# High and low parts of the rows as one 512-column operand in the FFN's first product, with its convolution taps read from SBUF

## The chip, the cores and the metric

The kernel runs on one core of a Trainium2 chip. The metric is the device time of one execution in microseconds (us); lower is better. Engines are called by the profile's names: PE is TensorE, DVE is VectorE, ACT is ScalarE, POOL is GpSimd, SP is SyncE, whose queue issues the weight loads.

## The reference, cut to what matters

One inference step of a hybrid backbone with four layers (mLSTM, windowed attention, neighbourhood attention, mLSTM) on 128 prompt tokens and 128 sample tokens, all in float32. Every layer ends with a gated feed-forward part (FFN) with a depthwise convolution of width 3 over the tokens between its first product and the gate:

```python
def _conv_ffn(h, w_up, conv_w, conv_b, w_down):
    u = _dwconv(h @ w_up, conv_w, conv_b)
    g, val = u[..., :D_FF], u[..., D_FF:]
    return (jax.nn.silu(g) * val) @ w_down
```

`D_MODEL` is 1024 and `D_FF` 2816, so `h @ w_up` is (256 x 1024) by (1024 x 5632) in each of the four layers, and the second product is (256 x 2816) by (2816 x 1024).

## The kernel before, in words

Activations lie transposed: features on the 128 partitions, the 256 tokens (two groups of 128, `TOK` in all) on the free axis. Every float32 product is made of three products of the narrower type float32r: a value is divided into a high part (`_hi`, a copy in float32r) and a low part (`_lo`, value minus high part), and w_hi·x_hi + w_hi·x_lo + w_lo·x_hi is summed in PSUM.

**Weights.** All weights are read once, in the order of use, as tiles of 1 MB (`stream`, 374 tiles) into a ring of four buffers `raw0` to `raw3`. SP issues the load of a tile into a buffer as soon as the tile that lay there has both its low halves made (`lo_done`), or, for the tiles of the conditioning product ("ada"), has been used by PE. Each other tile is split in two halves of 1024 columns: ACT writes the high part (`split_hi`, L446), DVE the low part (`split_lo`, L457), into a ring of `SPL` = 4 half-tile buffers `spl_hi` and `spl_lo`. A half-tile buffer comes free when PE has used the half (`half_used`), so the splits can be at most two tiles ahead of PE.

**FFN's first product.** For layer `i`, loop `j` runs over `NJ` = 11 pairs of tiles: tile `u` = 2j holds the weights of 256 gate features, tile 2j+1 those of 256 value features, each for all eight 128-row blocks of the input. `weights_stationary` (L534 to L536) does, for each of eight row blocks `k` and two blocks `b` of 128 features, three matmuls of 256 columns into one half of a PSUM bank: w_hi·H_hi, w_hi·H_lo, w_lo·H_hi; that is 48 matmuls a tile. `H_hi` and `H_lo` are the normalised input's parts, each 8 x 256 columns. The PSUM banks of the pair are `UP[0]`, `UP[1]` for even j and `ACC[2]`, `ACC[3]` for odd j.

**Behind the product.** ACT reads the finished bank and writes the middle tap with its bias to `tg` (gate) or `tv` (value) (`taps`, L1502, two instructions of 256 columns). DVE adds the two side taps, four `scalar_tensor_tensor` instructions for a tile, again with the PSUM bank as operand (`side_taps`, L1675 and L1679). ACT makes `sg` = silu(`tg`) (L1527), POOL multiplies `gt` = `sg`·`tv` (L2255), ACT writes `G_hi` (`gated_hi`), DVE writes `G_lo` (`gated_lo`, L2116). `G` is the operand of the second product, which `project` does (L585 to L587) in the same three-matmul form into `ACC[0]` to `ACC[3]`.

**Order.** Each engine's program is written out by hand in its own block, and its instructions run in that order; semaphores tie the engines. Per j, ACT's order is: split of tile 2j+1, taps of tile 2j, `gated_hi` of j-1, split of tile 2j+2, taps of tile 2j+1, silu. DVE's is: split of 2j+1, side taps of 2j, `gated_lo` of j-1, split of 2j+2, side taps of 2j+1. During layers 0 to 2 a few ada tiles (`fill`) run on PE between: one each after j = 2, 3 and 4, others around the norms. `norm` makes the input of each stage: DVE `hf` (L1626), POOL adds the shift (L2204), ACT `H_hi`, DVE `H_lo` (L1635), in four groups, and the first product's first tile waits for them group by group.

`H_hi`/`H_lo` are also read by the mLSTM's two input products (`weights_stationary`) and by the attention layers' `half_rows` (L567).

## Time and profile before

| | us |
|---|---|
| median of 3 runs | 1908.06 (1907.72 to 1908.47) |
| profiled execution | 1907.03 |
| its span in the trace | 1905.2 |

The profile page sums each engine's busy time over the span, cuts the span into 40 slices of 47.6 us, follows back the chain of work that ended last, and groups instructions by line. Durations of one instruction include its own start and end, so two that follow each other closely overlap in the record: where the pace matters, start times are compared, not durations. A matmul of 256 columns is recorded as 0.28 us long though the next one starts 0.12 us after it.

### The profile page before, as it was taken

The page shows a single profiled execution, that of the slowest core. Times are in us where ns is not written, and L with a number is a line of the kernel's source. Part 1 is how long each engine was busy: PE and PEld are TensorE (multiplying, and loading weights), DVE is VectorE, ACT ScalarE, POOL GpSimd, SP SyncE. Part 2 cuts the span into 40 slices and gives each one's busy share as a digit, 9 for nine tenths or more (in the row PEclk, how much of TensorE's full clock was granted, in tenths as well). Part 3 has the DMA queues.
Part 4 walks back from the last instruction along what each step waited for, and adds up shares of the span by engine and source line. Part 5 has one row for each costly group of instructions (what it writes and reads, how often), then busy time and mean ns, then how long its engine had stood idle before and what let it go on. Part 6 is the DMA issues. An engine that isn't in the chain of part 4 may idle for free.

```text
span 1905.2 us, 32196 instructions
## 1 busy us (share of the span) xinstructions
PE 1844.5 (97%) x13744; PEld 1652.7 (87%) x13744; DVE 1270.5 (67%) x1739; ACT 926.7 (49%) x1365; POOL 270.5 (14%) x198
## 2 busy tenths in 40 slices
PE   5999999999999999999999999999999999999998
PEld 2999877798999867999976789998998777989998
DVE  3854676667786666787455677856654776668874
ACT  2753445444554354555344455545643445446552
POOL 2100121011110122111111221102100220021211
PEclk8999999999999999999999999999999999999999
DMA  9555556857655767655573776556655647645551
GB/s 363 198 228 185 202 182 261 313 198 279 226 186 197 272 228 296 240 189 192 206 289 150 287 278 234 188 193 243 226 183 167 222 176 284 253 150 185 190 193 52
DMA packets 72543, 418.41 MB, mean 220 GB/s; under 512 B 12176, under 2 KB 18696, under 8 KB 24144
## 3 DMA queue, kind: packets, MB, share of 16 engines
q1 hardware_dynamic: 53856, 392.19, 55.4%
q10 hardware_dynamic: 18544, 24.17, 3.9%
q8 instruction: 108, 1.77, 0.4%
q14 instruction: 35, 0.29, 0.0%
HBM read 405.35 MB, written 10.95 MB: 218 GB/s over the span
## 4 chain that ended last, share of the span: by engine, by line
PE 87%; DVE 5%; DMA 2%; ACT 2%; issue 2%; POOL 2%; ACTq 0%; POOLq 0%; SPq 0%; DVEq 0%
PE ps L534 15%; PE ps L535 15%; PE ps L536 15%; PE ps L551 9%; PE ps L585 6%; PE ps L586 6%; PE ps L587 6%; PE ps L567 4%; PE ps L598 3%; DMA raw<-in_stream 2%; PE ps L801 1%; DVE spl_lo L457 1%; PE ps L786 1%; DMA out_new_C<-c_stage 1%; POOL hf L2204 1%
## 5 line engine op out<-in xcount | busy, mean ns | idle before, releaser
L457 DVE TENSOR_TENSOR spl_lo<-raw,spl_hi 128x1024 fp32r<-128x1024 f32 x556 | 726.8, 1342 | 249.2 <-ACT spl_hi L446 248.5
L446 ACT ACTIVATE spl_hi<-raw 128x1024 fp32r<-128x1024 f32 x556 | 565.1, 1053 | 305.5 <-PE ps L587 160.9
L534 PE MATMUL ps<-H_hi,spl_hi 128*128 128x256 f32 x1920 | 548.4, 286 | 8.3 <-DVE H_lo L1635 6.7
L535 PE MATMUL ps<-H_lo,spl_hi 128*128 128x256 f32 x1920 | 544.3, 283 | 0.0
L536 PE MATMUL ps<-H_hi,spl_lo 128*128 128x256 f32 x1920 | 544.2, 283 | 0.0
L534 PEld LDWEIGHTS ps<-H_hi,spl_hi 128*128 128x128 f32 x1920 | 369.4, 192 | 30.2 <-issue 30.1
L535 PEld LDWEIGHTS ps<-H_lo,spl_hi 128*128 128x128 f32 x1920 | 369.7, 193 | 0.1
L536 PEld LDWEIGHTS ps<-H_hi,spl_lo 128*128 128x128 f32 x1920 | 369.4, 192 | 0.0
L585 PE MATMUL ps<-G_hi,spl_hi 128*128 128x256 f32 x704 | 199.2, 283 | 0.0
L586 PE MATMUL ps<-G_lo,spl_hi 128*128 128x256 f32 x704 | 199.2, 283 | 0.0
L587 PE MATMUL ps<-G_hi,spl_lo 128*128 128x256 f32 x704 | 199.2, 283 | 0.0
L2255 POOL TENSOR_TENSOR gt<-sg,tv 128x512 f32<-128x512 f32 x44 | 92.7, 2106 | 439.9 <-DVE tv L1679 377.2
L534 PE MATMUL ps<-B_hi,spl_hi 128*128 128x256 f32 x512 | 145.0, 283 | 0.0
L535 PE MATMUL ps<-B_lo,spl_hi 128*128 128x256 f32 x512 | 144.9, 283 | 0.0
L536 PE MATMUL ps<-B_hi,spl_lo 128*128 128x256 f32 x512 | 144.9, 283 | 0.0
L585 PEld LDWEIGHTS ps<-G_hi,spl_hi 128*128 128x128 f32 x704 | 135.2, 192 | 0.0
L586 PEld LDWEIGHTS ps<-G_lo,spl_hi 128*128 128x128 f32 x704 | 135.2, 192 | 0.0
L587 PEld LDWEIGHTS ps<-G_hi,spl_lo 128*128 128x128 f32 x704 | 135.2, 192 | 0.0
L598 PE MATMUL ps<-raw,cond_wide 128*32 128x512 f32 x768 | 103.6, 644 | 20.4 <-DMA raw<-in_stream 10.8
L534 PEld LDWEIGHTS ps<-B_hi,spl_hi 128*128 128x128 f32 x512 | 98.3, 192 | 0.0
L536 PEld LDWEIGHTS ps<-B_hi,spl_lo 128*128 128x128 f32 x512 | 98.3, 192 | 0.0
L535 PEld LDWEIGHTS ps<-B_lo,spl_hi 128*128 128x128 f32 x512 | 98.3, 192 | 0.0
(237 smaller groups left out, 2754.2 us busy)
## 6 DMA issues: line engine op xcount, KB each, us to landing
raw<-in_stream SPq DMA_DIRECT2D x374, 1024.0 KB, 5.0
out_new_C<-c_stage ACTq DMA_DIRECT2D x16, 512.0 KB, 4.0
ada_b<-in_ada_b ACTq DMA_DIRECT2D x4, 768.0 KB, 9.9
E<-rows_out ACTq DMA_DIRECT2D x8, 256.0 KB, 4.5
Em<-rows_out ACTq DMA_DIRECT2D x8, 256.0 KB, 4.8
x<-in_x ACTq DMA_DIRECT2D x1, 1024.0 KB, 12.1
wide<-rows_out ACTq DMA_DIRECT2D x8, 128.0 KB, 5.5
cache<-in_na_cache ACTq DMA_DIRECT2D x1, 1024.0 KB, 7.9
```

The source lines that it names most:

```text
L446: act.activation(spl_hi[m % SPL][:, :], raw[r % RAW][:, h * HALF:(h + 1) * HALF], ACT.Copy).then_inc(S["hi_done"], 1)
L457: dve.tensor_tensor(spl_lo[m % SPL][:, :], raw[r % RAW][:, h * HALF:(h + 1) * HALF], spl_hi[m % SPL][:, :].bitcast(F32), ALU.subtract).the ...
L534: pe.matmul(out, w_hi, x_hi, start=st, stop=False, skip_group_check=True)
L535: pe.matmul(out, w_hi, x_lo, start=False, stop=False, skip_group_check=True)
L536: mm = pe.matmul(out, w_lo, x_hi, start=False, stop=en, skip_group_check=True)
L551: mm = pe.matmul(ACC[2 * s + c][:, :], a, w[m % SPL][:, c * 512:(c + 1) * 512], start=st, stop=en, skip_group_check=True)
L567: mm = pe.matmul(banks[s][:, :], a, w[m % SPL][:, k * 512:(k + 1) * 512], start=t == h == k == 0 and a is a_hi and w is spl_hi, stop=t == ...
L585: pe.matmul(out, w_hi, x_hi, start=st, stop=False, skip_group_check=True)
L586: pe.matmul(out, w_hi, x_lo, start=False, stop=False, skip_group_check=True)
L587: mm = pe.matmul(out, w_lo, x_hi, start=False, stop=en, skip_group_check=True)
L598: mm = pe.matmul(ADA_PS[32 * j:32 * j + ADA_M, 0:ADA_N], cond_wide[:, k * ADA_M:(k + 1) * ADA_M], raw[r % RAW][:, j * ADA_N:(j + 1) * ADA_ ...
L2255: pool.tensor_tensor(gt[j % 2][:, :], sg[j % 2][:, :], tv[j % 2][:, :], ALU.mult).then_inc(S["gt_done"], 1)
```

## The change: what it does

- `H_hi` and `H_lo` become one tensor `H` in which the high and low parts of each row block lie side by side: 256 columns high, 256 columns low. Its writers in `norm` write with a stride (`beside`), and the readers outside the FFN take their halves from it (`both_of`).
- The FFN's first product uses a new routine `wide_up`. For each row block and each block of 128 features it issues two matmuls in place of three: w_hi against all 512 columns (high and low part at once), and w_lo against the 256 high columns, accumulated on the first 256 of the 512 outputs. A feature block's output is now a whole bank, in two halves, and a tile takes two banks. Three such pairs of banks (`UPS`) are used in turn: `ps4`/`ps5`, `ps0`/`ps1`, `ps2`/`ps3`.
- The two halves of the output have to be added. ACT copies the high half of both banks to a new SBUF tile `up` (three buffers of 512 columns), DVE adds the low half from PSUM (`sum_up`). PE waits with tile u for the sum of tile u-3.
- The middle tap (ACT) and the side taps (DVE) read `up` in SBUF in place of the PSUM bank.
- The splits of tile u+2 are divided: its first half is split before the engine waits for tile u, its second half after the copy (ACT) or after the sum (DVE).
- The gate product `gt` = `sg`·`tv` moves from POOL to DVE, behind the side taps of the value tile.
- Not shown in the diff below: `split_hi` and `split_lo` get an argument that names the halves, two semaphores are added (`up_hi`, `up_sum`), and the three calls of `both(H_hi, H_lo)` outside the FFN become `both_of(H)`.

```diff
@@ -298,8 +298,7 @@
     x = sb("x", KD * TOK, F32, 64 * KB)
-    H_hi = sb("H_hi", KD * TOK, F32R, 72 * KB)
-    H_lo = sb("H_lo", KD * TOK, F32R, 80 * KB)
+    H = sb("H", 2 * KD * TOK, F32R, 72 * KB)
     rA, rB, rX, rT, rW = 88 * KB, 120 * KB, 152 * KB, 168 * KB, 184 * KB
@@ -340,6 +339,7 @@
                       for o, name in enumerate(("tg", "tv", "sg", "gt")))
+    up = [sb(f"up{b}", 2 * TOK, F32, rW + 2 * KB * b) for b in range(3)]
     G_hi = sb("G_hi", 2 * NJ * TOK, F32R, rA)
@@ -397,9 +397,11 @@
-    ps = [nc.alloc_psum_tensor(f"ps{b}", [P, 512], F32) for b in range(8)]
+    two = [nc.alloc_psum_tensor(f"ps{b}", [P, 1024], F32) for b in range(4)]
+    ps = [two[b // 2][:, 512 * (b % 2):512 * (b % 2) + 512] for b in range(8)]
     ACC, UP, ADA_PS, MISC = ps[0:4], ps[4:6], ps[6], ps[7]
     SCORES = (UP[1], MISC)
+    UPS = (two[2], two[0], two[1])
@@ -408,6 +410,13 @@
         return ap.rearrange("p (a b) -> p a b", b=b)
+    def halves(u):
+        return UPS[u % 3][:, :].rearrange("p (b e t) -> p b e t", e=2, t=TOK)
+    def beside(t, g, e):
+        return t[:, g * 1024:(g + 1) * 1024].rearrange("p (k e t) -> p k e t", e=2, t=TOK)[:, :, e]
@@ -536,6 +545,24 @@
+            def wide_up(n, banks, norm=None):
+                for h in range(2):
+                    m = 2 * n + h
+                    pe.wait_ge(S["lo_done"], m + 1)
+                    for k in range(4):
+                        kk = 4 * h + k
+                        if norm is not None and k % 2 == 0:
+                            pe.wait_ge(S["h_done"], 4 * norm + 2 * h + k // 2 + 1)
+                        for b in range(2):
+                            c = slice(k * 256 + b * P, k * 256 + b * P + P)
+                            w_hi, w_lo = spl_hi[m % SPL][:, c], spl_lo[m % SPL][:, c]
+                            pe.matmul(banks[:, b * 512:(b + 1) * 512], w_hi, H[:, kk * 512:(kk + 1) * 512], start=kk == 0,
+                                      stop=False, skip_group_check=True)
+                            mm = pe.matmul(banks[:, b * 512:b * 512 + TOK], w_lo, H[:, kk * 512:kk * 512 + TOK],
+                                           start=False, stop=kk == KD - 1, skip_group_check=True)
+                    mm.then_inc(S["half_used"], 1)
             def rows_stationary(n, chunk, first, last):
@@ -1048,14 +1078,12 @@
                 for j in range(NJ):
-                    k = NJ * i + j
-                    g_bank, v_bank = (ACC[2], ACC[3]) if j % 2 else (UP[0], UP[1])
-                    if j >= 2:
-                        pe.wait_ge(S["cg_done"], k - 1)
-                    weights_stationary(n0 + 2 * j, both(H_hi, H_lo), 0, g_bank, True, True, 2 * i + 1 if j == 0 else None)
-                    if j >= 2:
-                        pe.wait_ge(S["cv_done"], k - 1)
-                    weights_stationary(n0 + 2 * j + 1, both(H_hi, H_lo), 0, v_bank, True, True)
+                    for u in range(2 * j, 2 * j + 2):
+                        if u >= 3:
+                            pe.wait_ge(S["up_sum"], 2 * NJ * i + u - 2)
+                        elif u == 1 and i + 1 == DEPTH:
+                            pe.wait_ge(S["cn_evac"], 8 * MH)
+                        wide_up(n0 + u, UPS[u % 3], 2 * i + 1 if u == 0 else None)
                     if i + 1 < DEPTH:
@@ -1126,7 +1154,7 @@
                     act.wait_ge(S["hf_done"], 4 * q + g + 1)
-                    copy(H_hi[:, g * 512:(g + 1) * 512], hf[g % 2][:, :], "hhi_done")
+                    copy(beside(H, g, 0), v3(hf[g % 2][:, :], TOK), "hhi_done")
                     if late and g == 1:
@@ -1496,11 +1524,11 @@
-                def taps(dst, bank, j, blk, sem):
+                def taps(dst, u, blk, sem):
+                    act.wait_ge(S["up_sum"], 2 * NJ * i + u + 1)
                     for b in range(2):
-                        k = blk + 2 * j + b
-                        act.activation(dst[:, b * TOK:(b + 1) * TOK], bank[:, b * TOK:(b + 1) * TOK], ACT.Identity,
-                                       bias=small[:, b0 + k:b0 + k + 1],
+                        o, k = slice(b * TOK, (b + 1) * TOK), blk + u // 2 * 2 + b
+                        act.activation(dst[:, o], up[u % 3][:, o], ACT.Identity, bias=small[:, b0 + k:b0 + k + 1],
                                        scale=small[:, w0 + k:w0 + k + 1]).then_inc(S[sem], 1)
@@ -1510,22 +1538,28 @@
+                def high(u):
+                    split_hi(act, n0 + u + 2, (0,))
+                    tile_used(act, n0 + u)
+                    if 2 * NJ * i + u >= 3:
+                        done = NJ * i + (u - 3) // 2 + 1
+                        act.wait_ge(S[("cg_done", "cv_done")[(u - 3) % 2]], done)
+                    copy(v3(up[u % 3][:, :], TOK), halves(u)[:, :, 0], "up_hi")
+                    split_hi(act, n0 + u + 2, (1,))
+                split_hi(act, n0 + 1)
                 for j in range(NJ):
                     k = NJ * i + j
-                    g_bank, v_bank = (ACC[2], ACC[3]) if j % 2 else (UP[0], UP[1])
-                    split_hi(act, n0 + 2 * j + 1)
-                    tile_used(act, n0 + 2 * j)
-                    taps(tg[j % 2], g_bank, j, 0, "tg_done")
+                    high(2 * j)
+                    taps(tg[j % 2], 2 * j, 0, "tg_done")
                     if j:
                         gated_hi(j - 1)
-                    split_hi(act, n0 + 2 * j + 2)
-                    tile_used(act, n0 + 2 * j + 1)
+                    high(2 * j + 1)
                     if k >= 2:
                         act.wait_ge(S["gt_done"], k - 1)
-                    taps(tv[j % 2], v_bank, j, FB // 2, "tv_done")
+                    taps(tv[j % 2], 2 * j + 1, FB // 2, "tv_done")
                     act.wait_ge(S["cg_done"], k + 1)
                     act.activation(sg[j % 2][:, :], tg[j % 2][:, :], ACT.Silu).then_inc(S["sg_done"], 1)
-                split_hi(act, INDEX["ffn_down", i, 1])
                 gated_hi(NJ - 1)
@@ -1632,8 +1666,8 @@
                     dve.wait_ge(S["hhi_done"], 4 * q + g + 1)
-                    dve.tensor_tensor(H_lo[:, g * 512:(g + 1) * 512], hf[g % 2][:, :],
-                                      H_hi[:, g * 512:(g + 1) * 512].bitcast(F32), ALU.subtract).then_inc(S["h_done"], 1)
+                    dve.tensor_tensor(beside(H, g, 1), v3(hf[g % 2][:, :], TOK), beside(H, g, 0).bitcast(F32),
+                                      ALU.subtract).then_inc(S["h_done"], 1)
@@ -2116,23 +2150,35 @@
+                def sum_up(u):
+                    split_lo(dve, n0 + u + 2, (0,))
+                    dve.wait_ge(S["up_hi"], 2 * NJ * i + u + 1)
+                    t = v3(up[u % 3][:, :], TOK)
+                    dve.tensor_tensor(t, halves(u)[:, :, 1], t, ALU.add).then_inc(S["up_sum"], 1)
+                    split_lo(dve, n0 + u + 2, (1,))
+                split_lo(dve, n0 + 1)
                 for j in range(NJ):
                     k = NJ * i + j
-                    g_bank, v_bank = (ACC[2], ACC[3]) if j % 2 else (UP[0], UP[1])
-                    split_lo(dve, n0 + 2 * j + 1)
+                    sum_up(2 * j)
+                    dve.wait_ge(S["tg_done"], 2 * k + 2)
+                    side_taps(tg[j % 2], up[2 * j % 3], 2 * j, w0, w0 + 2 * FB, "cg_half", 2 * k + 2, "cg_done")
+                    if j:
+                        gated_lo(j - 1)
                     if i + 1 < DEPTH:
...
                             mod_columns(i + 1, 0)
-                    dve.wait_ge(S["tg_done"], 2 * k + 2)
-                    side_taps(tg[j % 2], g_bank, 2 * j, w0, w0 + 2 * FB, "cg_half", 2 * k + 2, "cg_done")
-                    if j:
-                        gated_lo(j - 1)
-                    split_lo(dve, n0 + 2 * j + 2)
+                    sum_up(2 * j + 1)
                     dve.wait_ge(S["tv_done"], 2 * k + 2)
-                    side_taps(tv[j % 2], v_bank, FB // 2 + 2 * j, w0, w0 + 2 * FB, "cv_half", 2 * k + 2, "cv_done")
-                split_lo(dve, INDEX["ffn_down", i, 1])
+                    side_taps(tv[j % 2], up[(2 * j + 1) % 3], FB // 2 + 2 * j, w0, w0 + 2 * FB, "cv_half", 2 * k + 2,
+                              "cv_done")
+                    dve.wait_ge(S["cv_done"], k + 1)
+                    dve.wait_ge(S["sg_done"], k + 1)
+                    if k >= 2:
+                        dve.wait_ge(S["ghi_done"], k - 1)
+                    dve.tensor_tensor(gt[j % 2][:, :], sg[j % 2][:, :], tv[j % 2][:, :], ALU.mult).then_inc(S["gt_done"], 1)
                 gated_lo(NJ - 1)
@@ -2246,13 +2292,6 @@
-                for j in range(NJ):
-                    k = NJ * i + j
-                    pool.wait_ge(S["sg_done"], k + 1)
-                    pool.wait_ge(S["cv_done"], k + 1)
-                    if k >= 2:
-                        pool.wait_ge(S["glo_done"], k - 1)
-                    pool.tensor_tensor(gt[j % 2][:, :], sg[j % 2][:, :], tv[j % 2][:, :], ALU.mult).then_inc(S["gt_done"], 1)
             norm(2 * DEPTH, shift=False)
```

## Rows read from the trace of the kernel before

**Rows 1.** The page: busy time of each engine, and the span in 40 slices.
```profile
PE 1844.5 (97%) x13744; PEld 1652.7 (87%) x13744; DVE 1270.5 (67%) x1739; ACT 926.7 (49%) x1365; POOL 270.5 (14%) x198
PE   5999999999999999999999999999999999999998
```

**Rows 2.** The page: chain of work that ended last, share of the span by engine.
```profile
PE 87%; DVE 5%; DMA 2%; ACT 2%; issue 2%; POOL 2%; ACTq 0%; POOLq 0%; SPq 0%; DVEq 0%
```

**Rows 3.** Stages: stretch, us, PE, PEld, DVE, ACT, POOL busy (instructions), PEclk, DMA share, GB/s.
```profile
442.90:574.20 131.30, 131.30 (x1093) 128.38 (x1090) 106.53 (x145) 75.13 (x109) 23.12 (x12) 1.00 0.61 225
1700.60:1830.50 129.90, 129.90 (x1071) 129.90 (x1072) 107.36 (x145) 76.80 (x113) 23.94 (x12) 0.99 0.51 180
```

**Rows 4.** Timeline of ACT in layer 0: start, us; taps of three tiles in turn.
```profile
568.08 1.02 ACT L1502 ACTIVATE tg<-ps,small 128x256 f32<-128x256 f32 x2 [2.33 <-PE ps L536]
569.52 2.00 ACT L446 ACTIVATE spl_hi<-raw 128x1024 fp32r<-128x1024 f32 x2
573.84 1.02 ACT L1502 ACTIVATE tv<-ps,small 128x256 f32<-128x256 f32 x2 [2.33 <-PE ps L536]
```

**Rows 5.** Timeline of PE, first product, layer 0: first and last of 57 matmuls.
```profile
454.72 0.28 PE L536 MATMUL ps<-H_hi,spl_lo 128*128 128x256 f32 x1
...
461.44 0.28 PE L535 MATMUL ps<-H_lo,spl_hi 128*128 128x256 f32 x1
```

**Rows 6.** Timeline of PE, mLSTM's value product: first start to last, ten pairs of matmuls.
```profile
200.02 0.62 PE L551 MATMUL ps<-spl_lo,A_hi 128*128 128x512 f32 x2
...
204.55 0.62 PE L551 MATMUL ps<-spl_hi,A_lo 128*128 128x512 f32 x2
```

**Rows 7.** Timeline of DVE over one pair j in layer 0; in brackets the idle time before.
```profile
563.38 0.87 DVE L1675 SCALAR_TENSOR_TENSOR tv<-ps,small,tv 128x254 f32<-128x254 f32 x2 [1.11 <-ACT tv L1502]
564.29 0.87 DVE L1679 SCALAR_TENSOR_TENSOR tv<-ps,small,tv 128x254 f32<-128x254 f32 x2
565.07 3.45 DVE L457 TENSOR_TENSOR spl_lo<-raw,spl_hi 128x1024 fp32r<-128x1024 f32 x2
569.14 0.87 DVE L1675 SCALAR_TENSOR_TENSOR tg<-ps,small,tg 128x254 f32<-128x254 f32 x2 [0.62 <-ACT tg L1502]
570.05 0.87 DVE L1679 SCALAR_TENSOR_TENSOR tg<-ps,small,tg 128x254 f32<-128x254 f32 x2
570.83 0.68 DVE L2116 TENSOR_TENSOR G_lo<-gt,G_hi 128x512 fp32r<-128x512 f32 x1
571.43 2.35 DVE L457 TENSOR_TENSOR spl_lo<-raw,spl_hi 128x1024 fp32r<-128x1024 f32 x2
```

**Rows 8.** Groups by line, all of the span: count, busy us, mean ns, idle before.
```profile
L1101 ACT ACTIVATE A_hi<-ps 128x512 fp32r<-128x512 f32 x16 | 9.6, 598 | 23.6 <-PE ps L536 23.6
L1842 DVE TENSOR_TENSOR E<-E,small 128x256 f32<-128x256 f32 x16 | 6.0, 417 | 0.0
L1986 DVE TENSOR_TENSOR O_lo<-ps,O_hi 128x256 fp32r<-128x256 f32 x16 | 6.8, 423 | 10.6 <-ACT O_hi L1101 10.6
L1857 DVE TENSOR_TENSOR den<-ps,den 128x512 f32<-128x512 f32 x8 | 5.5, 691 | 0.3
```

**Rows 9.** Waits of PE: who waited for whom, us in total, times, longest.
```profile
PE ps L534 <- DVE H_lo L1635: 6.7, 5, 2.7
PE ps L534 <- DVE spl_lo L457: 1.4, 5, 0.5
```

**Rows 10.** Timeline at the start of layer 3's FFN: its last low parts, its first tap.
```profile
1703.69 1.36 DVE L1635 TENSOR_TENSOR H_lo<-hf,H_hi 128x512 fp32r<-128x512 f32 x2 [1.20 <-ACT H_hi L1101]
1707.95 1.02 ACT L1502 ACTIVATE tg<-ps,small 128x256 f32<-128x256 f32 x2 [1.72 <-PE ps L536]
```

**Rows 11.** Stretches at the start of layer 1's FFN: PEclk, DMA share, GB/s.
```profile
752.00:754.00 2.00, 1.00 1.04 438
762.00:764.00 2.00, 1.00 1.05 436
```

More of the change, by code:

```diff
@@ L422, in build @@
         z_silu z_mul z_hi z_lo
-        tg_done cg_half cg_done tv_done cv_half cv_done sg_done gt_done ghi_done glo_done
+        up_hi up_sum tg_done cg_half cg_done tv_done cv_half cv_done sg_done gt_done ghi_done glo_done
         cache_landed bias_landed row_a row_d row_k row_v roped tq_mm tq_a tq_d tk_mm tk_a tk_d kv_landed
@@ L434, in landed, with split_hi @@
         eng.wait_ge(raw_landed[n % RAW], 16 * (n // RAW + 1))
-    def split_hi(act, n):
+    def split_hi(act, n, halves=(0, 1)):
         if n >= len(MAIN):
@@ L441, in split_hi @@
         landed(act, r)
-        for h in range(2):
+        for h in halves:
             m = 2 * n + h
@@ L447, in split_hi, with split_lo @@
                            ACT.Copy).then_inc(S["hi_done"], 1)
-    def split_lo(dve, n):
+    def split_lo(dve, n, halves=(0, 1)):
         if n >= len(MAIN):
@@ L453, in split_lo @@
         r = POS[MAIN[n]]
-        for h in range(2):
+        for h in halves:
             m = 2 * n + h
@@ L564, in half_rows @@
                         for s in range(NS):
-                            a_hi, a_lo = both(H_hi, H_lo)(4 * t + 2 * h + k, s)
+                            a_hi, a_lo = both_of(H)(4 * t + 2 * h + k, s)
                             for a, w in ((a_hi, spl_hi), (a_hi, spl_lo), (a_lo, spl_hi)):
@@ L622, in both, with both_of @@
                 return lambda k, s=None: (col(hi, k, s), col(lo, k, s))
+            def both_of(t):
+                return lambda k, s=None: (col(t, 2 * k, s), col(t, 2 * k + 1, s))
             def square_sums(q):
@@ L669, in mlstm @@
                     pe.wait_ge(S["conv_done"], 8 * j + t + 1)
-                    weights_stationary(n0 + t, both(H_hi, H_lo), 0, UP[t % 2], True, True,
+                    weights_stationary(n0 + t, both_of(H), 0, UP[t % 2], True, True,
                                        2 * i if t == 0 else None)
@@ L725, in gate_z @@
                     pe.wait_ge(S["z_silu"], 8 * j + t + 1)
-                    weights_stationary(INDEX["ml_z", i, t], both(H_hi, H_lo), 0, UP[t % 2], True, True)
+                    weights_stationary(INDEX["ml_z", i, t], both_of(H), 0, UP[t % 2], True, True)
                 pe.wait_ge(S["den_done"], 4 * (j + 1))
```

## The prediction

> **What bounds the kernel now.** I read the page first: PE is busy for 97% of the span and every slice but the first and the last has PE at 9 tenths [rows 1]. The chain that ended last runs over PE for 87% of the span; the rest is spread over five engines [rows 2]. Then the stage that is changed: in layer 0's first product PE is busy for all of the 131.3 us, DVE for 107, ACT for 75, and the same in layer 3 [rows 3]. The taps of successive tiles start 5.76 us apart, and ACT waits for PE each time [rows 4]; that is 48 matmuls at 0.120 us, the pace at which PE starts them: 56 steps in 461.44 - 454.72 = 6.72 us [rows 5]. So PE bounds the stage with no gap, at its full granted clock (1.00, 2.4 GHz) [rows 3]. A pair j takes 2 x 5.76 = 11.52 us.
>
> **PE: three matmuls become two.** The cost of a matmul is its pace, not its recorded length. 256 columns: 0.1200 us. At 2.4 GHz the columns alone are 0.1067, so 0.0133 is a part that belongs to each instruction. 512 columns, from the value product whose operands have the same types and the same 128 x 128 stationary: 20 matmuls in 204.55 - 200.02 = 4.53 us, 0.2265 each [rows 6]; the columns are 0.2133, and 0.0132 remains. So the fixed part is the same for both widths, and the change does the same columns (768) with one fixed part less. A group goes from 3 x 0.1200 = 0.3600 to 0.2265 + 0.1200 = 0.3465, a saving of 0.0135. There are 16 groups in a tile, 22 tiles in a layer, 4 layers: 1408 x 0.0135 = **19.0 us**. A tile goes from 5.76 to 5.544 us, a pair j to 11.09. No row has a 512-column matmul followed by a 256-column one with another stationary; from both sides the group costs between 0.333 (the next weights' load hides the fixed part in the longer stream, both parts gone: saving 38 us) and 0.360 or a little over (no saving). I take 0.3465, since its two halves are each measured.
>
> The Trainium skill (TensorE: Matmul & The Clock Gate, "Wait — 56ns, not 53.3ns?") gives a fixed cost of about 2.5 ns for a warm matmul. By that page the sum would be 1408 x 2.5 ns = 3.5 us, which would hardly be seen. This trace's rows show 13 ns instead, at both widths, and the sum goes by them.
>
> **What takes a part of it back.** The first tile of a layer waits for `H_lo` group by group [rows 9]. In layer 3 the last two low parts end at about 1704.4 and 1705.05, and the first tap starts at 1707.95 [rows 10], so that tile is paced by the norm and not by PE in its first half. There only the groups after the last wait are saved. I take 0.1 us lost a layer, **0.4 us**. Layers 1 and 2 start with the DMA engines full (438 and 436 GB/s) [rows 11]. A tile of 1 MB then takes 2.4 us, against 5.5 us for which PE works on one, and ACT's next wait in the stretch was for PE; the half split that is now earlier on ACT asks for a tile half a tile earlier. I cost it at nothing; the cover is the two tiles of lead that the four half buffers give. If it goes, the copy of tile u stands behind a wait for a load on ACT, 1 to 2 us in three layers, which the rotation of three bank pairs still hides.
>
> **DVE: does it keep up with 11.09?** From the starts over one j [rows 7]: 11.52 us, less the idle 1.11 and 0.62, is 9.79 us occupied. Removed: the two splits that run while POOL multiplies take 3.45 us, the two that do not 2.35, so moving the product off POOL gives DVE 1.10 back: 8.69. Added: two sums and one gate product of 512 elements. The row for this shape is `G_lo`, which occupies DVE from 570.83 to 571.43, 0.60 us; with a PSUM operand it is as long (691 ns for `den` against 682 for `G_lo`) [rows 7, 8]. So 3 x 0.60 = 1.80, and about 0.1 for the wait of the gate product on the side taps just before it: 10.6 us. Reading `up` in place of PSUM changes nothing for DVE: 417 ns from SBUF and 423 from PSUM for 256 elements [rows 8]. The bound on the other side is full durations with nothing overlapped, four splits at 1.23, eight taps at 0.478, four at 0.69 = 11.5. PE needs 11.09, and I take 10.6, by the row that shows the overlap: DVE has 0.5 us a pair left, and the work is hidden behind PE.
>
> **The waits that are new on DVE and ACT.** Behind PE's end of tile u: ACT copies (0.6 us, as in the copy of 512 columns from PSUM [rows 8]), DVE adds (0.7), meanwhile ACT splits the second half (1.0), DVE makes its low part (1.2, after a gap of 0.4 for ACT), ACT's two taps run beside that, DVE's side taps take 1.7. Queued behind DVE's wait for the copy are the low split of the second half and the side taps, for which PE waits later. The low part of half 1 of tile u+2 is ready 0.6 + 1.0 + 1.2 + small = 2.9 us after tile u; PE wants it after one and a half tiles, 8.3 us. The slack is 5.4 us. When DVE lags, ACT runs ahead with copy and split and the gap of 0.4 closes, so the chain doesn't repeat serially. PE's own new wait, for the sum of tile u-3, is two tiles (11 us) old when it comes. ACT: 75.1 us in 131.3 [rows 3], plus 22 copies of 0.6 and some 0.03 a tap = 90 in 122, no bound. SP: `raw` buffers are released about 2 us earlier than now. POOL is idle in the stage. In the pairs with `copy_mod` and `mod_columns` (j = 5 and 7) DVE has 0.7 to 0.8 more, that is 0.2 to 0.3 over one pair, taken up by the slack. After the last tile `G_lo` is complete about 6.6 us later (sum, split, side taps, product, high part, low part); the second product asks for it after two and a half tiles, 14.4 us. The writes to `H` with a stride change no element count: nothing, and if it were 0.1 us a group, 0.1 x 4 x 8 = 3 us on the path of the norms.
>
> **Sum.** 1907.03 - 19.0 + 0.4 = 1888.4 for an execution like the profiled one (span 1886.6). The median lies 1.03 above that execution, so 1889.5.
>
> **The rivals.**
> *Slower: DVE becomes the bound of the stage.* If a pair j takes x on DVE (or on the pair of ACT and DVE with their four hand-overs), a layer's first product takes 11x - 5.4 in place of 11 x 11.09. From x = 11.58 it costs something, from x = 12.0 all of the gain is gone. It would be 12.2 if no instruction overlapped (11.5 above) and both gaps of about 0.38 stayed: 4 x (11 x 1.11 - 5.4) = 27 us over the forecast, 1917. For it: DVE's busy time in the stage is 107 of 131 us already, and 1.8 us a pair are put on it. Against it: rows 7 show the overlap, and the POOL contention that goes. Chance 0.09.
> *Half of that: x between 11.6 and 12.0.* PE stalls in some pairs: 1890 to 1904. Chance 0.11.
> *The fixed part is not saved*, since it belongs to the hand-over between two stationaries or to the bank and the mixed widths pay it whole, or in truth it is near the page's figure: 0 to 3.5 us off, 1904.5 to 1908. For it: no row shows the mixture. Against: both widths show the same 13 ns. Chance 0.06.
> *The forecast*, 1887 to 1892: 0.71. *More than forecast* (the load of weights hides better beside 512 columns), 1870 to 1887: 0.03.
>
> **How the numbers follow.** About 0.2% (3.8 us) is what a measurement of this kernel can tell from no change, so faster means below 1904.2: 0.71 + 0.11 + 0.03 = 0.85. Same 0.06, slower 0.09. The range reaches from 1886 over the forecast and most of the half case to 1899; about 0.19 is left out.
>
> **What the profile of the changed kernel would show.** Matmuls of 512 and 256 columns in turn, starting 0.2265 and 0.120 apart; copies of ACT 5.54 us apart, each waiting for PE; PE busy in the whole of the stage, and the stage of layer 0 about 126.6 us in place of 131.3. Splits on DVE of 2.35 for two everywhere in it, none of 3.45; DVE busy about as now or a little more, with an idle rest of some 0.5 us a pair. The prediction is wrong if PE shows waits for `spl_lo` or `up` inside the stage (rival one, and their sum says how much), or if the groups start 0.36 us apart (the fixed part not saved).

## The result, and the profile after

The changed kernel takes 1893.15 us (median of 5, 1892.68 to 1898.71) against 1908.06. The ratio is 0.9923, with a 95% interval of 0.9913 to 0.9934: 14.7 us faster (12.6 to 16.6). It was forecast at 1889.5, with 1886 to 1899 as the range. So the direction and most of the size came as forecast, and about 4 us of the 18.6 are missing. The profiled execution is the slowest of the five (1898.71, span 1896.9), so the sum is not read from its span but stage by stage.

The page of the changed kernel: each engine's busy time (PEld is PE's loading of weights), and the two matmuls that took the place of three (line, engine, out<-in, shapes, count, busy us, mean ns, idle before).

```profile
PE 1835.8 (97%) x12336; PEld 1577.7 (83%) x12336; DVE 1312.5 (69%) x1871; ACT 980.9 (52%) x1453; POOL 177.7 (9%) x154
L560 PE MATMUL ps<-H,spl_hi 128*128 128x512 f32 x1408 | 497.5, 399 | 3.4 <-DVE H L1669 3.4
L562 PE MATMUL ps<-H,spl_lo 128*128 128x256 f32 x1408 | 393.9, 280 | 0.0
```

PE has the 1408 instructions less that the change removes [rows 1], and is as busy as before: it still bounds the kernel. In the stage (446 to 567 us, layer 0) the stretches show PE with no gap and DVE at 91%, where it was 81% [rows 3]:

```profile
446.00:567.00 121.00, 121.00 (x696) 102.69 (x697) 110.19 (x168) 85.23 (x124) 1.30 (x2) 1.00 0.62 237
```

The groups by line of the same stretch, DVE's and ACT's part:

```profile
L466 DVE TENSOR_TENSOR spl_lo<-raw,spl_hi 128x1024 fp32r<-128x1024 f32 x42 | 51.2, 1221 | 7.5 <-ACT spl_hi L455 7.3
L455 ACT ACTIVATE spl_hi<-raw 128x1024 fp32r<-128x1024 f32 x43 | 45.1, 1051 | 7.3 <-DMA raw<-in_stream 6.8 <-PE ps L562 0.2
L2157 DVE TENSOR_TENSOR up<-ps,up 128x512 f32<-128x512 f32 x20 | 13.7, 687 | 0.9 <-ACT up L1129 0.8
L2181 DVE TENSOR_TENSOR gt<-sg,tv 128x512 f32<-128x512 f32 x10 | 6.9, 693 | 0.3
```

The splits are at 1221 ns each, and none is stretched any more in any layer. DVE has 10.8 us idle in all (121.00 less 110.19), 7.5 of them before a split: about 1.0 us a pair. ACT waits 6.8 us for loads, which were costed at nothing; in layers 0 and 2 one copy comes 0.5 and 0.8 us late for that, and PE doesn't stall.

**Where the 4 us are.** ACT's copies mark the ends of tiles. Two places of layer 0, from the timeline of ACT (start, us, engine, line, operation):

```profile
463.10 0.60 ACT L1129 ACTIVATE up<-ps 128x512 f32<-128x512 f32 x1 [1.65 <-PE ps L562]
468.75 0.60 ACT L1129 ACTIVATE up<-ps 128x512 f32<-128x512 f32 x1 [1.66 <-PE ps L562]
...
545.74 0.60 ACT L1129 ACTIVATE up<-ps 128x512 f32<-128x512 f32 x1 [1.21 <-PE ps L562]
551.28 0.60 ACT L1129 ACTIVATE up<-ps 128x512 f32<-128x512 f32 x1 [1.34 <-PE ps L562]
```

Both wait for PE; the first pair is 5.65 us apart, the second 5.54. There are two paces. The timeline of PE, behind the first place and ahead of the second:

```profile
469.61 0.40 PE L560 MATMUL ps<-H,spl_hi 128*128 128x512 f32 x1
469.85 0.28 PE L562 MATMUL ps<-H,spl_lo 128*128 128x256 f32 x1
469.97 0.40 PE L560 MATMUL ps<-H,spl_hi 128*128 128x512 f32 x1
...
544.85 0.39 PE L560 MATMUL ps<-H,spl_hi 128*128 128x512 f32 x1
545.08 0.27 PE L562 MATMUL ps<-H,spl_lo 128*128 128x256 f32 x1
545.19 0.40 PE L560 MATMUL ps<-H,spl_hi 128*128 128x512 f32 x1
```

Averaged over the start times of 34 and of 97 groups, the 256-column matmul starts 0.2365 us after the 512-column one in the slow pace and 0.231 in the fast one, and the next 512-column one 0.117 and 0.1155 after it (starts are printed to 0.01 us; each part is good to about 0.001). A group takes 0.3533 or 0.3466 us. The forecast was 0.3465 everywhere. The loads of the weights do not tell the paces apart: in both each is recorded as 0.19 us long and starts within some 5 ns of a matmul's start. At the slow pace a tile keeps half of its gain. In this trace all of layer 3 is slow, layers 0 and 1 are slow up to the four transposes of the conditioning (`mod_rows`) after tile 13 and fast behind them, and layer 2 is fast at first, slow in the middle, fast at the end.

### The profile page after: what moved, and what is told of

It reads as the page before. It is cut to its first block, busy times and chain, and to the rows that moved or that the text cites. A ratio compares the mean times of both kernels' runs of the same rounds, so it can differ in the third digit from the quotient of the medians.

```text
span 1896.9 us, 29734 instructions
## 1 busy us (share of the span) xinstructions
PE 1835.8 (97%) x12336; PEld 1577.7 (83%) x12336; DVE 1312.5 (69%) x1871; ACT 980.9 (52%) x1453; POOL 177.7 (9%) x154
## 4 chain that ended last, share of the span: by engine, by line
PE 88%; DVE 5%; DMA 2%; ACT 2%; issue 2%; POOL 1%; ACTq 0%; POOLq 0%; SPq 0%; DVEq 0%
PE ps L560 17%; PE ps L578 9%; PE ps L562 9%; PE ps L612 6%; PE ps L614 6%; PE ps L613 6%; PE ps L543 6%; PE ps L545 6%; PE ps L544 6%; PE ps L594 4%; PE ps L625 3%; DMA raw<-in_stream 2%; DVE spl_lo L466 1%; PE ps L831 1%; PE ps L816 1%
## 5 line engine op out<-in xcount | busy, mean ns | idle before, releaser
L466 DVE TENSOR_TENSOR spl_lo<-raw,spl_hi 128x1024 fp32r<-128x1024 f32 x556 | 687.7, 1259 | 275.3 <-ACT spl_hi L455 274.3
L455 ACT ACTIVATE spl_hi<-raw 128x1024 fp32r<-128x1024 f32 x556 | 573.9, 1052 | 327.0 <-PE ps L614 161.5
L560 PE MATMUL ps<-H,spl_hi 128*128 128x512 f32 x1408 | 497.5, 399 | 3.4 <-DVE H L1669 3.4
L562 PE MATMUL ps<-H,spl_lo 128*128 128x256 f32 x1408 | 393.9, 280 | 0.0
L560 PEld LDWEIGHTS ps<-H,spl_hi 128*128 128x128 f32 x1408 | 265.0, 188 | 78.2 <-issue 14.6
L562 PEld LDWEIGHTS ps<-H,spl_lo 128*128 128x128 f32 x1408 | 266.1, 189 | 0.0
L543 PE MATMUL ps<-H,spl_hi 128*128 128x256 f32 x512 | 148.2, 289 | 6.8 <-DVE H L1669 5.2
L544 PE MATMUL ps<-H,spl_hi 128*128 128x256 f32 x512 | 146.0, 285 | 0.0
L545 PE MATMUL ps<-H,spl_lo 128*128 128x256 f32 x512 | 146.0, 285 | 0.0
L543 PEld LDWEIGHTS ps<-H,spl_hi 128*128 128x128 f32 x512 | 99.4, 194 | 16.6 <-issue 16.5
L1129 ACT ACTIVATE up<-ps 128x512 f32<-128x512 f32 x88 | 52.7, 599 | 115.5 <-PE ps L562 115.3
L544 PEld LDWEIGHTS ps<-H,spl_hi 128*128 128x128 f32 x512 | 99.5, 194 | 0.1
```

Source lines behind the costliest of these rows:

```text
L455: act.activation(spl_hi[m % SPL][:, :], raw[r % RAW][:, h * HALF:(h + 1) * HALF], ACT.Copy).then_inc(S["hi_done"], 1)
L466: dve.tensor_tensor(spl_lo[m % SPL][:, :], raw[r % RAW][:, h * HALF:(h + 1) * HALF], spl_hi[m % SPL][:, :].bitcast(F32), ALU.subtract).the ...
L543: pe.matmul(out, w_hi, x_hi, start=st, stop=False, skip_group_check=True)
L544: pe.matmul(out, w_hi, x_lo, start=False, stop=False, skip_group_check=True)
L545: mm = pe.matmul(out, w_lo, x_hi, start=False, stop=en, skip_group_check=True)
L560: pe.matmul(banks[:, b * 512:(b + 1) * 512], w_hi, H[:, kk * 512:(kk + 1) * 512], start=kk == 0, stop=False, skip_group_check=True)
```

## The experiments

"Stage sum" is the time from the first to the last copy of a layer (in the kernel before, to the last first tap), added over the four layers: 84 steps between tiles, with the fills and transposes that stand between them. It is 495.75 us in the kernel before and 483.2 in the first trace of the changed one. It leaves out everything that varies elsewhere; the spans outside it differ from trace to trace by up to 7 us (1408.3 to 1415.3) over all kernels, so times of single runs scatter by some 3 us either way. Each kernel has one trace; a pace is read from that one execution.

**The changed kernel again** (no edit). 

> The changed kernel once more. In its first trace the groups of two matmuls of the first product start 0.3533 us apart in some tiles (5.65 us a tile) and 0.3466 in others (5.55), and the pace changes only where PE did other work between. Theory A (the pace is set by how PE enters the stream of alternating widths, and holds until something interrupts it): this trace shows the same two values and no third, over long stretches, perhaps in other layers than before; runs lie between 1888.5 (all tiles at 0.3466) and 1898 (all at 0.3533), and the ratio is near 0.992. Theory B (slow tiles are slowed by what DVE and ACT do beside them): the same tiles are slow as before, since the work beside them is the same.

Measured: 1894.37 us (1892.93 to 1895.26), ratio 0.9921 (0.9909 to 0.9934). The stage sum is 480.6. The same two values, but in other places: layer 3, which was slow from end to end (118.7 us), is fast from end to end (116.5). Two of its copies (timeline of ACT), 5.54 us apart:

```profile
1739.94 0.60 ACT L1129 ACTIVATE up<-ps 128x512 f32<-128x512 f32 x1 [1.52 <-PE ps L562]
1745.48 0.60 ACT L1129 ACTIVATE up<-ps 128x512 f32<-128x512 f32 x1 [1.55 <-PE ps L562]
```

The instructions beside it are the same in both. Theory B falls in its simple form; the pace is a property of the execution, not of the tile.

**Three matmuls in the new layout.**

```diff
-                            pe.matmul(banks[:, b * 512:(b + 1) * 512], w_hi, H[:, kk * 512:(kk + 1) * 512], start=kk == 0,
-                                      stop=False, skip_group_check=True)
+                            pe.matmul(banks[:, b * 512:b * 512 + TOK], w_hi, H[:, kk * 512:kk * 512 + TOK], start=kk == 0,
+                                      stop=False, skip_group_check=True)
+                            pe.matmul(banks[:, b * 512 + TOK:(b + 1) * 512], w_hi, H[:, kk * 512 + TOK:(kk + 1) * 512],
+                                      start=False, stop=False, skip_group_check=True)
```

> The changed kernel, but with w_hi against 256 high columns and then 256 low columns in two matmuls in place of one of 512: three matmuls of 256 a group as in the kernel before, in the new layout, with the new banks, copies, sums, taps from SBUF and the product on DVE. Theory A (all of the gain is in the matmuls, all the rest is hidden behind PE): groups start 0.3600 us apart in every tile, 5.76 us a tile, and the time is that of the kernel before within 2 us, 1906 to 1910. Theory B (the new work on DVE and ACT costs PE something): slower than the kernel before by more than 2 us, or tiles of more than 5.76 us without a fill in them.

Measured: 1908.83 us (1906.62 to 1910.41), ratio 1.0004 (0.9995 to 1.0013), every tile without a fill at 5.76, stage sum 495.72 against 495.75. Two copies in layer 3 (timeline of ACT):

```profile
1744.16 0.60 ACT L1131 ACTIVATE up<-ps 128x512 f32<-128x512 f32 x1 [1.76 <-PE ps L564]
1749.92 0.60 ACT L1131 ACTIVATE up<-ps 128x512 f32<-128x512 f32 x1 [1.76 <-PE ps L564]
```

With the old matmuls all the rest of the change (copies, sums, taps from SBUF, product on DVE, interleaved `H`, divided splits, three bank pairs) is worth nothing in either direction, within 2 us. The whole gain is the instruction that is left out of each group. With one width only there is one pace.

**The order of the matmuls: by two, by four, by eight.** All 512-column matmuls of one, two or four row blocks first, then the 256-column ones; for one row block:

```diff
                         for b in range(2):
...
-                            pe.matmul(banks[:, b * 512:(b + 1) * 512], w_hi, H[:, kk * 512:(kk + 1) * 512], start=kk == 0,
-                                      stop=False, skip_group_check=True)
-                            mm = pe.matmul(banks[:, b * 512:b * 512 + TOK], w_lo, H[:, kk * 512:kk * 512 + TOK],
-                                           start=False, stop=kk == KD - 1, skip_group_check=True)
+                            pe.matmul(banks[:, b * 512:(b + 1) * 512], spl_hi[m % SPL][:, c], H[:, kk * 512:(kk + 1) * 512],
+                                      start=kk == 0, stop=False, skip_group_check=True)
+                        for b in range(2):
+                            c = slice(k * 256 + b * P, k * 256 + b * P + P)
+                            mm = pe.matmul(banks[:, b * 512:b * 512 + TOK], spl_lo[m % SPL][:, c], H[:, kk * 512:kk * 512 + TOK],
+                                           start=False, stop=kk == KD - 1, skip_group_check=True)
```

> The order of the matmuls alone is changed: for each row block the two of 512 columns first (both banks), then the two of 256 columns. Theory A: the slow pace comes from the change of width; with half as many changes of width either the slow pace is 0.0033 us a group dearer than the fast one in place of 0.0067, or it doesn't occur at all; 1888.5 to 1893. Theory B (work beside): the same two paces, 0.3533 and 0.3466, in the same tiles; 1893. A third possibility, that two matmuls of 512 in a row leave less room to load weights, would give a pace above 0.3533, 1899 or more.

> The order of the matmuls alone: of two row blocks the four of 512 columns first, then the four of 256. In pairs (two and two) a group took 0.3483 us in every tile, where the alternating order takes 0.3466 or 0.3533. Theory C (the sum of the two widths' own paces, 0.2265 and 0.1200, holds within a run of one width, and every change of width costs something fixed): half the surplus of 0.0017 is left, 0.3474 a group, 5.56 us a tile in all tiles, and no second pace. If the surplus doesn't depend on the number of changes: 0.3483 again. Time 1889 to 1894.

> The same with a whole half tile: eight of 512 columns, then eight of 256. By theory C 0.3470 a group, 5.552 us a tile in all tiles. The first tile of a layer has to wait for four groups of the norm at once and loses up to 1.4 us a layer where PE waits for them (the first tile in layer 3 above all). Time 1889 to 1894.

| order | us (median, range) | ratio (interval) | tile, us | group, us | stage sum |
|---|---|---|---|---|---|
| alternating, first trace | 1893.15 (1892.7 to 1898.7) | 0.9923 (0.9913 to 0.9934) | 5.65 or 5.55 | 0.3533 or 0.3466 | 483.2 |
| by two | 1897.65 (1891.7 to 1898.1) | 0.9932 (0.9920 to 0.9945) | 5.573 | 0.3483 | 480.3 |
| by four | 1898.02 (1896.5 to 1898.3) | 0.9938 (0.9925 to 0.9950) | 5.613 | 0.3508 | 483.3 |
| by eight | 1897.67 (1896.7 to 1899.5) | 0.9939 (0.9927 to 0.9952) | 5.587 | 0.3492 | 480.6 |

Each of the three has a single pace in its trace, so the second pace belongs, as far as these traces go, to the strict alternation. Theory C falls: fewer changes of width make a group dearer (by four) and not cheaper, and none reaches the fast alternating pace. That pace is the sum of the two single widths' own (0.3465 [rows 5, 6]), so grouping by width has nothing to give here. All three times lie above what was expected for them (at most 1893, 1894 and 1894). They are not shown to differ from the alternating order either: the intervals of the ratios overlap, and the stage sums lie, to 0.1 us, among those of the alternating kernels without added work (478.6 to 483.2). Whether the time outside the stage has a part in it is open (1413.3 to 1415.3 us in these three traces, 1409.6 to 1413.7 in the alternating ones without added work); by four and by eight also make the first tile of a layer wait for two or four groups of the norm at once.

**The order within a group turned**: w_lo against 256 columns, then w_hi against 512 (the two `matmul` calls change places, with the start flag). 

> The order within a group is turned: w_lo against 256 columns first, then w_hi against 512. A stream of alternating widths as before, so by theory A two paces again, 0.3466 and 0.3533 a group, with changes only where other PE work stands between; 1890 to 1897. If the second pace belongs to the order in which the same PSUM columns are written, there is one pace only.

Measured: 1894.37 us (1891.90 to 1897.35), ratio 0.9926 (0.9911 to 0.9941). Two paces again, 5.66 only in the first tiles of layer 1, 5.55 elsewhere; with 478.6 the shortest stage sum of all: 17.1 us less than before, of 17.9 that would be there with all 84 steps fast. It shows what the forecast's term is worth when the pace holds. Its traced execution is the fastest of its four (1891.90); the median shows no difference from the order as it was. The second pace does not belong to the order within a group.

**Other PE work between the tiles.** In layer 3 no fill stands between tiles, so its pace ought to change only where something is put in.

```diff
                         wide_up(n0 + u, UPS[u % 3], 2 * i + 1 if u == 0 else None)
+                        if i + 1 == DEPTH and u in NUDGE:
+                            pe.wait_ge(S["modT_done"], 3 * DEPTH)
+                            for b in range(NUDGE[u]):
+                                pe.transpose(ADA_PS[:, b * P:(b + 1) * P], ident, ident)
```

`NUDGE` is `{3: 1, 6: 1, 9: 2, 12: 2, 15: 4, 18: 4}`. 

> In layer 3 alone, where no other PE work stands between the tiles, PE does 1, 1, 2, 2, 4 and 4 transposes of 128 columns into an unused bank after tiles 3, 6, 9, 12, 15 and 18. They cost about 0.06 us each, 0.9 us in all. Theory A (entry into the stream sets the pace): the tiles' distance changes between 5.65 and 5.55 us at some of these places and at no other. Theory B (work beside them): it stays at 5.65 through all of layer 3, as in the first trace.

Measured: 1896.29 us (1893.16 to 1897.04), ratio 0.9928 (0.9913 to 0.9943). ACT's copies around the two places with two transposes (timeline of ACT, layer 3):

```profile
1744.34 0.60 ACT L1134 ACTIVATE up<-ps 128x512 f32<-128x512 f32 x1 [1.55 <-PE ps L563]
...
1749.88 0.60 ACT L1134 ACTIVATE up<-ps 128x512 f32<-128x512 f32 x1 [1.52 <-PE ps L563]
...
1755.76 0.60 ACT L1134 ACTIVATE up<-ps 128x512 f32<-128x512 f32 x1 [1.71 <-PE ps L563]
...
1761.41 0.60 ACT L1134 ACTIVATE up<-ps 128x512 f32<-128x512 f32 x1 [1.66 <-PE ps L563]
...
1772.85 0.60 ACT L1134 ACTIVATE up<-ps 128x512 f32<-128x512 f32 x1 [1.65 <-PE ps L563]
1778.39 0.60 ACT L1134 ACTIVATE up<-ps 128x512 f32<-128x512 f32 x1 [1.55 <-PE ps L563]
```

5.54 apart ahead of the first place, 5.88 over it, 5.65 behind it, and 5.54 again behind the second. One transpose left the pace as it was (two of two), two changed it (two of two), four led to the slow pace, from the fast one and from the slow one. A transpose cost 0.11 us, and not 0.06 as expected. In layer 3 the pace changed nowhere else. That bears out theory A: other work of PE can change the pace, and it then holds until something interrupts the stream. Whether it is the kind of work or only the length of the interruption is not separated here.

**Four transposes with an increment.** 

> After the first tile of every layer, and in layer 3 after tiles 7 and 14 too, PE does four transposes of 128 columns into an unused bank, the last with a semaphore increment, as the transposes of the conditioning (mod_rows) have it after tile 13 of layers 0 to 2. In the seven traces of the alternating order looked at so far, all 21 stretches behind mod_rows ran at 5.55 us a tile, though the tiles before ran at either pace, while four transposes without an increment left 5.65 in both of two cases. Theory D (the increment, or four transposes ended in this way, puts PE into the fast pace): 5.55 behind each of the six places. Theory A alone (any entry, either pace by chance): both values among the six. The transposes cost some 0.4 us each time, 2.4 us in all; time 1890 to 1898.

Measured: 1897.93 us (1894.44 to 1898.84), ratio 0.9944 (0.9928 to 0.9961). Behind the six places: slow in layers 0, 1 and 2, fast behind the first in layer 3, slow behind the other two. Theory D falls. Behind `mod_rows` the pace was fast once more, in 24 of 24 stretches of the eight traces (in that of `load1`, below, for one step, until DVE set the pace). An entry that took either pace by chance would not do that, and what makes this one different is open. Four transposes cost 0.44 us each time. Had they forced the fast pace, they would have gained 0.1 us net over the five tiles up to the first fill in layers 0 to 2, and 1.8 us in layer 3, where all of it slow takes 118.7 us and all of it fast 116.5.

**More work on DVE.** Behind the sum of each tile:

```diff
                     dve.tensor_tensor(t, halves(u)[:, :, 1], t, ALU.add).then_inc(S["up_sum"], 1)
+                    dve.tensor_tensor(ow[1][:, :], x[:, 0:512], x[:, 512:1024], ALU.add)
```

> The changed kernel with one more DVE instruction of 512 elements for each tile, behind the sum (its output is used by nothing), 0.6 us or 1.2 us a pair. The prediction has DVE occupied for x = 10.6 us a pair and says that PE begins to lose at x = 11.58, with 4 x (11 x (x - 11.09) - 5.4) us. By it x = 11.8 and the load costs 9.6 us over the changed kernel, somewhat less since PE's tiles took 5.60 us on the mean in the traces so far (5 us at 11.2 a pair): 1898 to 1904. If DVE has in truth more room than that (x of 10.2 or less without the load), nothing is lost and the time is 1892 to 1896. If DVE were already the bound, the whole load would show: 88 x 0.6 = 53 us.

Measured: 1899.73 us (1897.43 to 1902.71), ratio 0.9954 (0.9938 to 0.9971), 6.6 us over the changed kernel's median (6 us by the ratios). Tiles run at 5.55 or 5.65 us up to about the eighth (layer 3) or the sixteenth (layers 0 to 2) and at 5.84 from there. The timeline of DVE over one pair in layer 3, from one sum to the next but one:

```profile
1746.84 0.69 DVE L2157 TENSOR_TENSOR up<-ps,up 128x512 f32<-128x512 f32 x1
1747.44 0.69 DVE L2159 TENSOR_TENSOR ow<-x 128x512 f32<-128x512 f32 x1
1748.03 1.22 DVE L466 TENSOR_TENSOR spl_lo<-raw,spl_hi 128x1024 fp32r<-128x1024 f32 x1
1749.17 0.88 DVE L1709 SCALAR_TENSOR_TENSOR tv<-up,small,tv 128x254 f32<-128x254 f32 x2
1750.08 0.88 DVE L1713 SCALAR_TENSOR_TENSOR tv<-up,small,tv 128x254 f32<-128x254 f32 x2
1750.99 0.69 DVE L2183 TENSOR_TENSOR gt<-sg,tv 128x512 f32<-128x512 f32 x1
...
1758.51 0.68 DVE L2157 TENSOR_TENSOR up<-ps,up 128x512 f32<-128x512 f32 x1
```

No row has a bracket, nor has any of those left out: DVE is never idle for 0.15 us or more, and a pair takes 1758.51 - 1746.84 = 11.67 us. Less the two added instructions at 0.60 that is x = 10.47; the forecast put 10.6. A stretch a little later in the same layer is a warning:

```profile
1770.00:1820.00 50.00, 49.98 (x286) 43.31 (x284) 49.58 (x78) 34.31 (x52) 0.00 (x0) 1.00 0.49 177
```

PE is busy for 49.98 of 50 us although DVE sets its pace: the waits are shorter than the tail by which one recorded matmul overlaps the next (a 512-column one is recorded as 0.40 us long, the next starts after 0.23). "PE has no gap" doesn't show by itself that PE is the bound; the distance of its tiles does.

The same with one instruction of 1024 elements (`spare[:, :]` from `x[:, 0:1024]` and `x[:, 1024:2048]`). 

> The same with one instruction of 1024 elements for each tile, 1.1 to 1.2 us or 2.3 us a pair. By the prediction's formula x = 12.9 and the cost is 4 x (11 x 1.8 - 5.4) = 58 us over the changed kernel, 1950, and in the stage DVE has no idle time and PE waits for spl_lo or up. With room of another 0.5 us a pair it would be 35 us, 1928.

Measured, one run: 1941.51 us, 48 over the changed kernel's median; a pair takes 12.74 us in the trace (tiles of 6.37). From the waits of PE:

```profile
PE ps L561 <- DVE spl_lo L467: 17.6, 33, 0.8
```

Only here does a wait for DVE inside the stage become visible. x without the load is 12.74 - 2 x 1.13 = 10.5 once more.

**The product back on POOL** (the block removed from POOL's program put back, DVE's instruction taken out). 

> The changed kernel with the gate product back on POOL. DVE loses 0.7 us of work a pair and gets back the 1.1 that its splits lose while POOL multiplies: x = 11.0 by the prediction, still below 11.09. Theory A: PE bounds the stage either way, the time is that of the changed kernel within 2 us (1891 to 1896), and the splits of 1.7 us a piece are back in the trace. Rival: the move is worth something on the path since x is over 11.6 without it; then slower by 3 us or more, with waits of PE for spl_lo inside the stage.

Measured: 1892.35 us (1890.86 to 1896.85), ratio 0.9924 (0.9907 to 0.9941): no difference, as theory A has it. But its second half is mostly wrong: of the 38 stretched splits of the kernel before (over 1.5 us, in the four stages) 4 are back, none in layers 0 and 3. One line's summary (min/median/max ns), in the kernel before over layer 0's stage and here, and POOL and DVE beside each other here:

```profile
L457 DVE TENSOR_TENSOR spl_lo<-raw,spl_hi x44: 1212/1220/2320, 446.2 to 572.6; 128x1024 fp32r<-128x1024 f32 x44
```

```profile
L466 DVE TENSOR_TENSOR spl_lo<-raw,spl_hi x44: 1215/1221/1226, 447.0 to 566.1; 128x1024 fp32r<-128x1024 f32 x44
541.61 2.17 POOL L2296 TENSOR_TENSOR gt<-sg,tv 128x512 f32<-128x512 f32 x1 [9.56 <-DVE tv L1713]
541.39 1.22 DVE L466 TENSOR_TENSOR spl_lo<-raw,spl_hi 128x1024 fp32r<-128x1024 f32 x1
542.96 0.69 DVE L2157 TENSOR_TENSOR up<-ps,up 128x512 f32<-128x512 f32 x1 [0.35 <-ACT up L1129]
543.91 1.23 DVE L466 TENSOR_TENSOR spl_lo<-raw,spl_hi 128x1024 fp32r<-128x1024 f32 x1 [0.25 <-ACT spl_hi L455]
```

The split that starts 0.2 us ahead of POOL's product takes its 1.22 us; the next DVE instruction in POOL's 2.17 us is the sum, which has an operand in PSUM, and it takes its 0.69. The next split starts when POOL has ended. In the kernel before, two splits followed each other there, and the second started inside POOL's instruction and took 2.32. The same happens here in layer 1, where a split starts 0.15 us behind POOL; and in layer 0 there is a product with no split beside it (a second POOL row of this trace):

```profile
812.28 1.29 POOL L2296 TENSOR_TENSOR gt<-sg,tv 128x512 f32<-128x512 f32 x1 [11.30 <-DVE tv L1713]
812.43 2.22 DVE L466 TENSOR_TENSOR spl_lo<-raw,spl_hi 128x1024 fp32r<-128x1024 f32 x1 [0.28 <-ACT spl_hi L455]
481.71 1.30 POOL L2296 TENSOR_TENSOR gt<-sg,tv 128x512 f32<-128x512 f32 x1 [9.14 <-DVE tv L1713]
```

So it is an instruction that starts while POOL works and reads two operands in SBUF that is held up. And it goes both ways: POOL's product takes 1.3 us by itself and 2.15 when a split is already running as it starts, in nearly all pairs of the kernel before. The Trainium skill says so (SBUF — State Buffer, "Who interferes with whom": a VectorE instruction with two SBUF inputs contends with a GpSimd instruction that reads SBUF), and these traces agree: 2.32 us against 1.22 for the split, and 0.69 for the sum with its PSUM operand. In the new order of DVE the move off POOL returns next to nothing; it costs DVE 0.6 to 0.7 us a pair, which PE covers.

**Undivided splits.**

```diff
-                    split_hi(act, n0 + u + 2, (0,))
                     tile_used(act, n0 + u)
...
-                    split_hi(act, n0 + u + 2, (1,))
+                    split_hi(act, n0 + u + 2)
```

and the same for `split_lo` around the sum. 

> The changed kernel with the splits undivided: both halves of tile u+2 behind the copy and behind the sum. The low part of half 0 comes 1.1 us later, with 2.8 us less slack, since PE wants it after one tile. Theory A: hidden, same time within 2 us (1891 to 1896), the DVE's idle time a little longer. Rival: the divided split is what keeps PE fed, then PE waits for spl_lo, 3 us or more slower.

Measured: 1893.71 us (1892.26 to 1896.42), ratio 0.9928 (0.9914 to 0.9943), stage sum 482.3: no difference. The division is worth nothing as long as PE is the bound.

## Why the prediction was right, and where it was off

- **PE bounds the stage and the gain is in the matmuls:** shown, by `three` (1.0004 with the old matmuls and all the rest new).
- **The fixed part of 0.0133 us an instruction, 1408 of them, 19.0 us:** that a group with one instruction less is cheaper is right; this is the term that was mis-sized. It assumed that the paces measured in streams of one width add up in a mixed stream. In the fast pace they do (0.3466 against 0.3465), but by a sum whose parts are not the forecast's: the starts lie 0.231 and 0.1155 apart, where 0.2265 and 0.120 were forecast, and none of the other patterns gives the sum (0.3483, 0.3508, 0.3492, and 0.3533 in the slow pace, where only 0.0067 is saved). How exactly the fast pace meets it may be luck. In the traces of the alternating order that have no added work the stage sums are 12.5, 15.2, 13.5, 13.5 and 17.1 us under the kernel before's, 14.4 on the mean; the forecast has 18.1 for these 84 steps. The 3.8 us between them are about the 4 us that the time misses. The prediction said that no row had the mixture and gave 0.333 to 0.360 as the ends, and took the middle for likely. It did not think of two values in one execution. Layer 0's first product was forecast to take 4.7 us less (126.6 in place of 131.3); from its first matmul to the start of ACT's first work on its last tile it takes 127.6 in place of 131.0, 3.3 less.
- **The 2.5 ns a matmul of the Trainium skill** (TensorE: Matmul & The Clock Gate, "Wait — 56ns, not 53.3ns?"): an estimate of 3.5 us by that page. The stage gained 12.5 to 17.1. The rows decided rightly.
- **DVE at x = 10.6:** 10.5 by `load1` and `load2`. Its parts were not all right: the 1.1 us were counted as returned by moving the product; without the move nearly all of them would have come back too, through the new order. The loss beyond the slack was mis-sized at its lower end. At x = 11.67 the formula gives 4 us with PE at 11.09 a pair and nothing with PE at the 11.2 it really took; 6 to 7 were measured. At 12.74 it gives 51 and 46; 48 were measured. The lead of 5.4 us a layer is what is too large: in layer 3 of `load1` the tiles slow down after eight steps, when DVE has fallen behind by 8 x (5.84 - 5.55) = 2.3 us, and in `load2` by 3.1 us. In the other layers, as an estimate from the same steps, the fills between the tiles (1.2 us of PE's time each) let DVE catch up, which the formula leaves out.
- **What is hidden:** copies, taps, ACT's waits for loads, the divided split: at nothing, and nothing, within 2 us, is what `three` and `whole` show. The writes to `H` with a stride were not tested by themselves; `three` contains them. The prediction read [rows 11] as the starts of layers 1 and 2; both rows are of layer 1.
- **The 0.4 us taken for the first tiles:** too small to be shown. PE's waits for the norm's low parts in the stage are 0.55 and 2.67 us before (layers 2 and 3) and 0.75 and 2.67 after (layers 1 and 3); layer 3's first tile takes 7.36 us from its first matmul before and 7.44 after.
- **The rivals:** the slower one needed x over 12.0, and `load1` and `load2` show where DVE decides (11.7 costs 6 us, 12.7 costs 48). What happened lies between the forecast's own band and the rival in which the fixed part is not saved: half of that came true, in 9 to 60% of the tiles of a trace. No rival had that; the range held it because it was made wide for a slow DVE, and so the range is right in part by luck.

What stays open: what decides between the paces when PE enters the stream, and whether an order exists that always takes the fast one.

## What to carry to other kernels

Where PE is the bound and its matmuls are short, one instruction with a wider operand in place of two saves part of the cost of one, here 13 ns in one pace and 7 in the other, if the sum of the two halves can be made on engines that have time; price it by start times of the same shapes, not by recorded durations. A stream that mixes widths has to be measured as a mixture. To see how near a second engine is to becoming the bound, add a known load to it: the distance of the tiles then gives its full occupation, where busy shares (91%, and PE at 100%) do not.

## What the runs showed of the hardware that was not expected

- Matmuls of 512 and 256 columns in strict alternation, each with a new 128 x 128 stationary, run at 0.3466 or 0.3533 us a group at the same granted clock (1.00). The pace holds for up to a whole layer (116.5 or 118.7 us), changes in these traces only where other PE work stands between, and differs from one execution to the next. Behind one such place, four transposes with a wait and an increment, it was fast in 24 of 24 stretches.
- The same matmuls grouped by width run at one pace each, 0.3483, 0.3508 and 0.3492 us a group, always dearer than the fast alternation.
- DVE's long split (two SBUF operands) took up to 2.32 us only when it started inside a POOL instruction; started 0.2 us ahead of it, it took 1.22, and then POOL's product took 2.15 us in place of 1.3.
